# A hybrid attention and state-space decoder step: d_skip in rows, squares added first, whole tiles, two raw slots, and a fourth weight slot in the norm stage

## The reference

```
mod = silu(c) @ w_ada + b_ada                       # 2048 x 6144, for 9 conditioning rows
shift, scale, gate = split(mod, 3)
h = rmsnorm(x, g_pre) * (1 + scale) + shift
q, k, v, z_a, z_b, xbc, dt_raw, r_a, r_b = split(h @ w_in, cuts)
# A) dilated sliding-window attention, 8 heads of 128, groups (window, dilation) = (128,1), (512,4), (2048,16)
scores = einsum('bdnqhe,bdnkhe->bdnhqk', qs, kb) * ATT_SCALE      # masked to the window
o = einsum('bdnhqk,bdnkhe->bdnqhe', softmax(scores), vb)
p_a = (sum over groups of wts * o) * silu(z_a) @ w_o_a
# B) Mamba-2: conv over x/B/C, 8 groups, 32 heads of 64, state 128, chunked scan
y, new_ssm = _ssd(xs, dt, a, bm, cm, ssm_state)
y = y + xs * d_skip[:, None]
yg = y * silu(z_b)                                   # reshaped to 8 groups of 256
yg = yg * rsqrt(mean(yg * yg, axis=-1) + eps)
p_b = (yg * g_ssm) @ w_o_b
out = (sigmoid(r_a) * p_a + sigmoid(r_b) * p_b) @ w_o
y_out = x + gate * rmsnorm(out, g_post)
```

## Time and profile before

| what | us |
|---|---|
| time, median of 3 runs (lowest to highest) | 3129.91 (3122.58 to 3134.31) |
| the profiled execution's own time | 3134.02 |
| span of its instructions | 3132.2 |
| TensorE busy | 3016.7 (96%) |
| VectorE busy | 2036.4 (65%) |
| POOL busy | 1099.2 (35%) |
| ACT busy | 847.8 (27%) |

### The profile page before, as it was taken

The page is one execution under the profiler, slowest core; times in us unless marked ns, Lnnn a source line. Parts: engine busy times, 40 slices in busy tenths (PEclk is TensorE's granted clock), DMA queues, the critical chain, the costliest instruction groups (busy, mean ns, idle before and its releaser), DMA issues. The chain is left out here.

```text
span 3132.2 us, 52927 instructions
## 1 busy us (share of the span) xinstructions
PE 3016.7 (96%) x23068; PEld 2848.9 (91%) x23068; DVE 2036.4 (65%) x2027; ACT 847.8 (27%) x1026; POOL 1099.2 (35%) x368
## 2 busy tenths in 40 slices
PE   5899999999999999999999999999999999999996
PEld 4798999899999999999999999999999989999785
DVE  3301799998994988988888766887777854212202
ACT  2111222232323223233222133333333332212221
POOL 0133233333322333333343343444444423333332
PEclk8899999999999999999999999999999999999998
DMA  8768786654445786646667566666556655766643
GB/s 316 282 245 312 293 300 243 221 201 140 150 134 192 259 292 235 208 180 236 252 238 248 187 228 218 223 217 231 197 196 229 222 193 198 280 248 235 240 170 113
DMA packets 222396, 704.89 MB, mean 225 GB/s; under 512 B 28675, under 2 KB 131835, under 8 KB 172731
## 3 DMA queue, kind: packets, MB, share of 16 engines
q1 hardware_dynamic: 159622, 471.33, 43.9%
q0 software_dynamic: 5248, 174.60, 14.0%
q10 hardware_dynamic: 57296, 55.59, 5.3%
HBM read 630.85 MB, written 245.17 MB: 280 GB/s over the span
## 5 line engine op out<-in xcount | busy, mean ns | idle before, releaser
L1310 PE MATMUL acc<-act,w_hi 128*128 128x288 f32 x5808 | 1742.5, 300 | 18.0 <-POOL w_lo L866 17.9
L1311 PE MATMUL acc<-act,w_hi 128*128 128x288 f32 x5808 | 1715.1, 295 | 0.0
L1312 PE MATMUL acc<-act,w_lo 128*128 128x288 f32 x5808 | 1715.0, 295 | 0.0
L866 POOL TENSOR_TENSOR w_lo<-w_raw,w_hi 128x2048 fp32r<-128x2048 f32 (+1 forms) x209 | 958.0, 4584 | 1986.7 <-ACT w_hi L918 1986.5
L1310 PEld LDWEIGHTS acc<-act,w_hi 128*128 128x128 f32 x5808 | 1092.5, 188 | 43.6 <-issue 20.7
L1311 PEld LDWEIGHTS acc<-act,w_hi 128*128 128x128 f32 x5808 | 1092.7, 188 | 1.8
L1312 PEld LDWEIGHTS acc<-act,w_lo 128*128 128x128 f32 x5808 | 1091.6, 188 | 0.7
L918 ACT ACTIVATE w_hi<-w_raw 128x2048 fp32r<-128x2048 f32 (+1 forms) x209 | 384.7, 1841 | 512.4 <-PE acc L1312 194.4
L1722 DVE TENSOR_TENSOR side<-side 128x2048 f32<-128x2048 f32 x96 | 323.7, 3372 | 70.9 <-DMA side<-in_vals_t 57.8
L1693 DVE TENSOR_TENSOR side<-side 128x2048 f32<-128x2048 f32 x96 | 334.3, 3482 | 51.1 <-DMA side<-in_keys_t 47.2
L984 ACT ACTIVATE ev<-acc 128x576 f32<-128x576 f32 x144 | 93.7, 651 | 787.9 <-PE acc L1312 776.4
(11 more groups left out here) (291 smaller groups left out, 2683.1 us busy)
## 6 DMA issues: line engine op xcount, KB each, us to landing
w_raw<-in_w_in_t SPq DMA_DIRECT2D x160, 1024.0 KB, 7.7
out_s_kv<-in_cache_a_w POOLq DMA_DIRECT2D x80, 1632.0 KB, 9.0
side<-in_keys_t SPq DMA_DIRECT2D x52, 1024.0 KB, 7.3
side<-in_vals_t SPq DMA_DIRECT2D x52, 1024.0 KB, 7.4
w_raw<-in_w_ada_t SPq DMA_DIRECT2D x48, 1024.0 KB, 7.6
out_s_kv<-in_cache_a_w POOLq DMA_DIRECT2D x24, 1344.0 KB, 8.6
w_raw<-in_w_o_b_t SPq DMA_DIRECT2D x16, 1024.0 KB, 7.2
w_raw<-in_w_o_t SPq DMA_DIRECT2D x16, 1024.0 KB, 9.0
```

Of the source, the lines that this page charges most:

```text
L866: nc.gpsimd.tensor_tensor(wl[:, u % 2, 0:kt, 0:cols], raw[:, SLOT[s], 0:kt, 0:cols], wh[:, u % 2, 0:kt, 0:cols].bitcast(F32), ALU.subtract ...
L1310: nc.tensor.matmul(out, wh[:, c, k, 0:cols], high, start=(k == 0), stop=False)
L1311: nc.tensor.matmul(out, wh[:, c, k, 0:cols], low, start=False, stop=False)
L1312: mm = nc.tensor.matmul(out, wl[:, c, k, 0:cols], high, start=False, stop=(k == kt - 1))
```

## The change

1. **Fourth slot.** Entries up to `NADA` of the stream (the 32 `w_ada` tiles and unit 0) rotate over four slots. The fourth, `fourth`, lies in the side buffer at columns 15744 to 17792, with a semaphore `w_in3` of its own.
2. **Two raw slots from unit 18.** `_few` holds from `NGATE + 2` = 18 on instead of `BLOCK0` = 111, so the third slot is not loaded between units 17 and 165. At unit 165 the rotation restarts with slot 2. `seen`, the number of half-steps that SP lets pass before it goes on, has the lag 6 in place of 8 in units 18 to 110.
3. **Whole tiles.** `BAND`, the list of five parts of the banded 128 x 512 score tile, is gone. Every step makes the scores in one 128 x 512 matmul, and the values in four full ones instead of five parts. VectorE adds a mask of -1e30 outside the window to the whole score tile before the maximum and the exponential, before and after.
4. **d_skip in rows.** The host lays `d_skip` out as 128 x 16 (`d_skip_t`). One DMA of rows of 64 bytes takes the place of two that read it value by value and broadcast it to 64 partitions each. `const_in` counts 160 in place of 176.
5. **Squares added first.** VectorE adds `ysq[:, 1]` to `ysq[:, 0]` at o = 18 and signals `ysum`; TensorE waits for that and makes one matmul for each half in place of two.

```diff
@@ -139,13 +139,17 @@
 ENTRY.update({s: ("a", n) for n, s in enumerate(ADA_SLOT)})
 SLOT, BEFORE, LOADS = [], [], []
 _next = [0, 0]
+PSLOTS = 4
 for _s in range(NADA + len(STREAM)):
     _kind, _n = ENTRY[_s]
-    _few = _kind == "u" and BLOCK0 <= _n < A0 + 4
-    if _few:
-        _slot = _next[1] % 2
-        _next[1] += 1
+    _few = _kind == "u" and NGATE + 2 <= _n < A0 + 4
+    if _s <= NADA:
+        _slot = _s % PSLOTS
+    elif _few:
+        _slot = (_n + A0) % 2
     else:
+        if _kind == "u" and _n == A0 + 4:
+            _next[0] = 2
         _slot = _next[0] % 3
         _next[0] += 1
     _before = [i for i in range(_s) if SLOT[i] == _slot]
@@ -197,7 +201,6 @@
 NCH = len(DCHUNKS)
 
 ATT0 = 61
-BAND = ((0, 0, 64), (2, 64, 128), (1, 32, 64), (1, 64, 96), (3, 96, 128))
 PACE = 4
 KEYS0 = 20
 
@@ -312,6 +315,12 @@
         part = side[:, 15456:15712].rearrange("p (a n) -> p a n", a=2)
         pick = side[:, 15712:15712 + NSEQ]
         hF = ev
+        fourth = side[:, 15744:15744 + D].rearrange("p (k n) -> p k n", n=P)
+
+        def slot(s):
+
+            return fourth if SLOT[s] == 3 else raw[:, SLOT[s], :, :]
+
         bgate = side[0:NSEQ, 10208:10208 + D]
         grow = side[0:NSEQ, 10208 + D:10208 + 2 * D]
 
@@ -516,9 +525,9 @@
                 s = ADA_SLOT[n]
                 if n == EARLY:
                     weights(0)
-                if s >= 3:
+                if s >= PSLOTS:
                     slot_free(s)
-                sp.dma_start(raw[:, SLOT[s], :, :].rearrange("p k n -> p (k n)"), A["w_ada_t"][(n % 2) * KT + n // 2]).then_inc(w_in[SLOT[s]], 16)
+                sp.dma_start(slot(s).rearrange("p k n -> p (k n)"), A["w_ada_t"][(n % 2) * KT + n // 2]).then_inc(w_in[SLOT[s]], 16)
 
             sp.dma_start(causal[:, :], A["causal"]).then_inc(const_in, 16)
 
@@ -648,9 +657,7 @@
                     sp.dma_start(hv[:, 1:2], A["a_log"].rearrange("a h -> h a")).then_inc(const_in, 16)
                     sp.dma_start(blockm, A["block"]).then_inc(const_in, 16)
                     sp.dma_start(owner, A["owner"]).then_inc(const_in, 16)
-                    with nc.allow_non_contiguous_dma(reason="one value a descriptor, once"):
-                        for hh in range(2):
-                            sp.dma_start(dsk[64 * hh:64 * hh + 64, :], A["d_skip"][0:1, hh:SH:2].to_broadcast((64, KT))).then_inc(const_in, 16)
+                    sp.dma_start(dsk, A["d_skip_t"]).then_inc(const_in, 16)
                 if half == 2 * BLOCK0 + 8:
                     sp.wait_ge(dt_d, 5)
                     sp.dma_start(S["csT"], csv).then_inc(cs_out, 16)
@@ -774,7 +781,7 @@
 
             def seen(u):
 
-                lag = 8 if u < BLOCK0 else 6 if u < A0 + 2 else 2 if u < A0 + 4 else 4
+                lag = 8 if u < NGATE + 2 else 6 if u < A0 + 2 else 2 if u < A0 + 4 else 4
                 return max(0, 2 * min(u, NGATE + 2) - 4, 2 * u - lag)
 
             for u in range(NU + 4):
@@ -1206,7 +1213,7 @@
 
                 for k in range(KT):
                     q = 32 * (k % 4)
-                    mm = nc.tensor.matmul(ps_s[q:q + 32, (n % 2) * 512:(n % 2) * 512 + P], c32[:, k, :], raw[:, SLOT[src], k, :],
+                    mm = nc.tensor.matmul(ps_s[q:q + 32, (n % 2) * 512:(n % 2) * 512 + P], c32[:, k, :], slot(src)[:, k, :],
                                           start=(k < 4), stop=(k >= KT - 4))
                 mm.then_inc(ada_used, 1)
 
@@ -1344,12 +1351,7 @@
                         pe.wait_ge(qk_in, 16 * h + 16)
                     if n:
                         pe.wait_ge(at_pc, n)
-                    if n == 0:
-                        nc.tensor.matmul(ps_s[:, 0:512], qk[:, 0, r:SEQ:4], qk[:, 3, :], start=True, stop=True)
-                    else:
-                        for x, i0, i1 in BAND:
-                            nc.tensor.matmul(ps_s[i0:i1, x * P:(x + 1) * P], qk[:, 0, 4 * i0 + r:4 * i1:4], qk[:, 3, x * P:(x + 1) * P],
-                                             start=True, stop=True)
+                    nc.tensor.matmul(ps_s[:, 0:512], qk[:, 0, r:SEQ:4], qk[:, 3, :], start=True, stop=True)
                     nc.tensor.matmul(ps_s[:, 512:640], qk[:, 1, r:SEQ:4], qk[:, 4, r:SEQ:4], start=True, stop=True)
                     nc.tensor.matmul(ps_s[:, 640:768], qk[:, 2, r:SEQ:4], qk[:, 5, r:SEQ:4], start=True,
                                      stop=True).then_inc(at_sc, 1)
@@ -1368,8 +1370,8 @@
                     if r == 0:
                         pe.wait_ge(va_in, 48 * h + 48)
                     nc.tensor.matmul(ps_w[:, P:2 * P], pT[:, 4, :], vP[:, 4 + r, :], start=True, stop=False)
-                    for x, i0, i1 in BAND:
-                        nc.tensor.matmul(ps_w[i0:i1, P:2 * P], pT[:, x, i0:i1], vP[:, x, :], start=False, stop=False)
+                    for x in range(4):
+                        nc.tensor.matmul(ps_w[:, P:2 * P], pT[:, x, :], vP[:, x, :], start=False, stop=False)
                     nc.tensor.matmul(ps_w[:, P:2 * P], pT[:, 5, :], vP[:, 8 + r, :], start=False, stop=True).then_inc(at_o, 1)
 
             def fold_halves():
@@ -1495,14 +1497,12 @@
                         mm = nc.tensor.transpose(Y[:, j * P:(j + 1) * P], St[:, j * P:(j + 1) * P], ident[:, :])
                     mm.then_inc(st_t, 1)
                 if o == 18:
-                    pe.wait_ge(ysq_d, g + 1)
+                    pe.wait_ge(ysum, g + 1)
                     pe.wait_ge(st_c, g + 1)
                     pe.wait_ge(sn_a, 4 * g + 4)
                     pe.wait_ge(pool_set, 2)
                     for half, bank in enumerate((Y, Z)):
-                        for j in range(2):
-                            mm = nc.tensor.matmul(bank[:, 0:HALF], ones[:, :], ysq[:, j, half * HALF:(half + 1) * HALF],
-                                                  start=(j == 0), stop=(j == 1))
+                        mm = nc.tensor.matmul(bank[:, 0:HALF], ones[:, :], ysq[:, 0, half * HALF:(half + 1) * HALF], start=True, stop=True)
                     mm.then_inc(ss_t, 1)
 
             def last_b():
@@ -2007,6 +2007,9 @@
                     dve.wait_ge(yd, 10 * g + 10)
                     dve.wait_ge(evac, EVACS[UNIT["s", g, 1]])
                     TT(yT, yT, zs, ALU.mult).then_inc(yz, 1)
+                if o == 18:
+                    dve.wait_ge(ysq_d, g + 1)
+                    TT(ysq[:, 0, :], ysq[:, 0, :], ysq[:, 1, :], ALU.add).then_inc(ysum, 1)
                 if o == 19:
                     dve.wait_ge(rt, 2 * g + 2)
                     nc.vector.reciprocal(rst, rst).then_inc(yr, 1)
@@ -2192,6 +2195,7 @@
         keys[s] = rows[:, :, 0].reshape(NB, 2, 4, 16, H, E).transpose(2, 1, 0, 4, 3, 5).reshape(4, P, 16 * E)
         vals[s] = rows[:, :, 1].reshape(NB, 2, 64, H, 4, 32).transpose(4, 1, 0, 3, 5, 2).reshape(4, P, 32 * 64)
     out["keys_t"], out["vals_t"] = keys, vals
+    out["d_skip_t"] = np.ascontiguousarray(np.repeat(inputs["d_skip"][0].reshape(KT, 2).T, P // 2, axis=0))
     for name in ("w_o_a", "w_o_b"):
         out[name + "_t"] = tiles(inputs[name][0])
     out["w_o_t"] = np.ascontiguousarray(inputs["w_o"][0].reshape(4, 4, P, OG, 512).transpose(3, 0, 2, 1, 4)).reshape(KT, P, 4 * 512)
```

More of the change, by code:

```diff
@@ L416, in phase_all @@
         c_in, v_in, x_in, const_in = sems("c_in", "v_in", "x_in", "const_in")
-        w_in, ra_in = sems("w_in0", "w_in1", "w_in2"), sems("ra_in0", "ra_in1", "ra_in2")
+        w_in, ra_in = sems("w_in0", "w_in1", "w_in2", "w_in3"), sems("ra_in0", "ra_in1", "ra_in2")
         c_act, c_t, v_t, set_up, pool_set = sems("c_act", "c_t", "v_t", "set_up", "pool_set")
@@ L442, in phase_all @@
         st_t, st_c, p_out = sems("st_t", "st_c", "p_out")
-        yz, ysq_d, ss_t, rt, yr, yn, y_out = sems("yz", "ysq_d", "ss_t", "rt", "yr", "yn", "y_out")
+        yz, ysq_d, ysum, ss_t, rt, yr, yn, y_out = sems("yz", "ysq_d", "ysum", "ss_t", "rt", "yr", "yn", "y_out")
         ma_d, mr_in, mr_d = m.sem("ma_d"), sems("mr_in0", "mr_in1"), m.sem("mr_d")
@@ L843, in ssm @@
                     if g == 0:
-                        pool.wait_ge(const_in, 176)
+                        pool.wait_ge(const_in, 160)
                     nc.gpsimd.tensor_tensor(Bm, Bt[0:SAMP, 0, :].unsqueeze(1).broadcast_to((SAMP, NB, P)),
@@ L1854, in dt_part @@
                 if half == 2 * BLOCK0 + 5:
-                    dve.wait_ge(const_in, 176)
+                    dve.wait_ge(const_in, 160)
                     dve.wait_ge(evac, EVACS[u])
@@ L2153 @@
          "c_prompt", "c_sample", "b_ada", "g_pre", "g_post", "conv_w", "conv_b", "dt_bias", "a_log",
-         "d_skip", "g_ssm")
+         "g_ssm")
 OUTS = (("y_prompt", (1, SEQ, D)), ("y_sample", (NB, NT, D)),
```

## The result

The changed kernel takes 3098.19 us, median of 4 runs (3093.83 to 3102.36), against 3130.52 for the kernel before (4 runs, 3122.58 to 3134.31): ratio 0.9898, 95% interval 0.9882 to 0.9914. That is 32 us less, 1.0%. In a second comparison the same kernel gave 0.9902 (0.9889 to 0.9915). The forecast was 3106 with a range of 3094 to 3120, so the time lies inside it.

A forecast was written before the change was run, and what follows sets the result against it. TensorE was taken as the bound, busy 3016.7 of 3132.2 us, leaving 115 us of gaps or TensorE work itself. Terms summed to -23.6: 3110.4 from the profiled 3134.0, 3106.3 from the median; forecast 3106, range 3094 to 3120.

The forecast's parts named there:

- Fourth slot, -10: Norm stage: three loads in flight instead of two end the last `w_ada` use at 114.8; -10 us, from -14 to -4.
- unit 18, +1: Unit 18's load now waits for the last gate tile, so its first matmul comes at 404.1 against 403.18: +1 us.
- Rival (a): Norm stage gives back 3 us instead of 10, as a faster feed meets TensorE at half clock: 3113; chance 0.15.
- Two slots, 0: From unit 18, weight loads issued one unit later still land in time: 0 us, upper end +3.
- the other side: The prediction's case for a slower kernel, full matmul passes costing load plus move: 3153 us; chance 0.06, half of it slower.
- Scores -4.3: Attention scores as whole tiles take 1.66 us instead of 1.80, for each of 31 steps: -4.3 us.
- values -1: Attention's weighted values in full passes, twelve a step, save 0.03 us in each of 32 steps: -1 us, from -2 to +6.
- Rival (c): Attention values: full passes cost load plus move, 0.235 us each, +46 us, 3153; chance 0.06, half of it slower.
- d_skip, -7.6: Around 1810 to 1827 us: TensorE's 4.25 us wait and 3.3 us of lower clock both go; -7.6 us, at least -4.
- Rival (d): POOL's cache copies, not d_skip, held the weight load, so the wait at 1827 stays: 3114; chance 0.07.
- Squares, 0: Sum of squares: 0.97 us saved a group, eaten by a 1.1 us wait in six of eight; 0, from -7.8 to +6.
- Block end, -1.7: From unit 165, A tiles are issued sooner, so the wait of 1.74 us at 2599.92 goes: -1.7 us.

The follow-up runs named there:

- norm3: The changed kernel with three slots instead of four in the norm stage: 3113.53 us, ratio 0.9943 to the kernel before.
- fourth_alone: The kernel before with the fourth slot in the norm stage and nothing else of the change: 3115.30 us, ratio 0.9956.
- the undo: The changed kernel with d_skip read value by value again, in two transfers of four-byte descriptors: 3109.58 us, ratio 0.9928 to the kernel before.
- restart_0: The changed kernel with unit 165 going to slot 0 as before, instead of slot 2: 3108.83 us, ratio 0.9927 to the kernel before.
- three_to_110: The changed kernel with three raw slots up to unit 110 and SP's lag of before: 3105.31 us, ratio 0.9924 to the kernel before.
- three_lag6: The changed kernel with three raw slots up to unit 110 but its own shorter lag: 3103.45 us, ratio 0.9914 to the kernel before.

## Why the prediction was right, point by point

The sign was right, the range held, and the size was a quarter too small: -23.6 was forecast against a profiled execution of 3134.0, and the spans differ by 34.4; against the medians 24 was forecast and 32 came. Term by term:

- **Fourth slot, -10, and unit 18, +1**: right in mechanism, a little small. The last tile is used at 113.94 to 115.0 (forecast 114.8). Together they measured -13.2 by unit 20 (-16.4 in the second profile); norm3 and fourth_alone give 11.7 and 13.3. The end at 115.0 does not show the two parts of its sum: 32 tiles in 92.9 us are 2.90 each, and whether that is 2.8 and a hold by TensorE, as I had it, or loads that came at 2.9 throughout, is not separated. What I took off for unit 1 did not come: its tile, issued at 115.08, landed in 4.9 us, not in the median 7.7, likely because the queues had run empty (a DMA share of 0.40 in 110:115); and unit 18's, issued at 376.1, landed in 4.8. The rule on the HBM side of the Trainium skill, DMA: Bandwidth & Descriptors, "Where 436 GB/s comes from", is met by the mean (355 GB/s over 20:126 now), though not by single stretches (374 in the earlier trace rows). Rival (a) is out.
- **Two slots, 0**: right, but for half a reason, and in that much by luck. The weight tiles landed in time. That SP's queue holds the key and value chunks too I left out of the sum, and the shorter lag, which stands in the diff and to which I gave no price, is worth 230 us. With it the term is 0; without it the change would have been 6% slower. That was the other side, and I had put it on the matmul passes, where there was nothing.
- **Scores -4.3, values -1**: measured -4.1 and -0.8. Rival (c) is out: a full pass takes (722.20 - 721.96)/2 = 0.12, with row groups that do not differ. By the rule about row groups of the Trainium skill, TensorE: Matmul & The Clock Gate, "Part 3: Packing small matmuls", a pass would take its load and its move one after the other; here the record of one weight load of L1374 is 0.19 long, and the next begins 0.11 later, so loads overlap the running matmuls. From 34 to 100 the changed kernel is 6.6 shorter than before. The other 1.7 stand at units 86 to 89, with waits on L1360 and L1339 (0.9), and are no gain of the change: its second profile has them again.
- **d_skip, -7.6**: measured 8.3 (8.2 in the undo). From 1773 to 1819 TensorE is busy throughout at a clock of 1.00, where before it lost 5.4 us of 53 and ran at 0.94. Rival (d) is out.
- **Squares, 0**: measured 1.35 lost in six groups (0.23 each, 0.15 forecast) and 0.97 won in two, -0.6 in all. The lock of the Trainium skill, SBUF — State Buffer, "SBUF: two separate sides", agrees with the row: an add that takes 0.75 alone (the shortest of the eight) took 4.0 in six of them, and 1.8 in group 6.
- **Block end, -1.7**: the term that was mis-sized. It measured -6.5 (8.4 from 160 to 180, less 1.9 of squares), and 5 to 8 by restart_0. I took the one wait that the list of waits names for L1310, and left out what follows from the same late tiles: another gap that is put down to other causes, and the clock that falls behind the gaps.

The sum fell 10.8 us short of the spans' difference: block end 4.8, norm stage 4.2, attention stretch 1.3, d_skip 0.7, squares 0.6, and 0.6 behind unit 180, less 1.4 given back on the way to unit 34. Of this the attention stretch's 1.3 and part of the norm stage and the block end lie within what two executions of one kernel differ by. The medians differ by 32.3, since the profiled execution of before was 3.5 us over its median.

## What to carry to other kernels

When a slot or a wait moves in a queue that issues in order, price what stands behind it in that queue, not the transfer alone: here the weight tiles had room and the chunks behind them did not, which was worth 230 us against 0. A cause of gaps is worth more than the wait that bears its name: the stretch's busy time and granted clock, read in windows, gave 5.7 us where the wait said 1.7. And what an engine loses to a wait may come back in part where the two engines meet next; measure it behind that place.

## What the runs showed that I had not expected

- The effect of a moved phase: VectorE's product of 2.28 us took 6.25 and 6.65 beside POOL's instruction when POOL began first, and 2.28 when the product did (POOL then took 6.17). TensorE lost 7 us in all to it, in two of three kernels with the same slots.
- The wait at the first attention step is 7.6 us in most kernels, also in norm3 and before, which come there as late as three_to_110. It is 2.9 in three_to_110 and three_lag6, the two in which TensorE had lost 7 us to VectorE at unit 18: some 5 us of that loss come back here. A shift of the norm stage as a whole does not.
